# The reciprocal root of 24 RMS norms: a square root on ScalarE and a reciprocal on VectorE for a logarithm and an exponential

## The reference

```
def rms_norm(x, g):
    xf = x.astype(jnp.float32)
    y = xf * lax.rsqrt(jnp.mean(xf * xf, axis=-1, keepdims=True) + EPS)
    return (y * g.astype(jnp.float32)).astype(x.dtype)
...
    o = rms_norm(o, g_out) * jax.nn.silu(r.reshape(B, L, GLA_HEADS, GLA_DV).astype(jnp.float32))
...
    for l in range(DEPTH):
        a = rms_norm(h, p['g_mix_pre'][l])
...
        h = h + rms_norm(m, p['g_mix_post'][l])
...
        f, c_new = conv_ffn(rms_norm(h, p['g_ffn_pre'][l]), prev, p['w_up'][l], p['conv_w'][l],
                            p['conv_b'][l], p['w_down'][l])
        new_conv.append(c_new)
        h = h + rms_norm(f, p['g_ffn_post'][l])
```

## Time and profile before

| | us |
|---|---|
| median of 3 runs | 2798.29 |
| lowest and highest | 2792.39, 2800.5 |
| profiled execution | 2794.6 |
| its span | 2792.8 |

### The profile page before, as it was taken

The page is one execution under the profiler, slowest core; times in us unless marked ns, Lnnn a source line. Parts: engine busy times, 40 slices in busy tenths (PEclk is TensorE's granted clock), DMA queues, the critical chain, the costliest instruction groups (busy, mean ns, idle before and its releaser), DMA issues.

```text
span 2792.8 us, 37637 instructions
## 1 busy us (share of the span) xinstructions
PE 2521.1 (90%) x15437; PEld 2206.9 (79%) x15437; DVE 1654.8 (59%) x2811; ACT 1140.4 (41%) x1792; POOL 85.5 (3%) x22
## 2 busy tenths in 40 slices
PE   2999999998999999999997889878999999999994
PEld 1777888887778879999995666667777888999994
DVE  2677556665665555765555666665665555655554
ACT  2555444343443324333334656553443333333232
POOL 0000000000010000010000110000001000000000
PEclk8999999988999999999998899989999999999997
DMA  7222213322422323323223222221332232332222
GB/s 153 78 67 76 84 63 101 106 85 81 155 78 96 98 76 96 133 74 99 84 84 100 74 90 76 67 93 34 107 129 91 93 98 79 106 118 80 88 91 75
DMA packets 93799, 255.17 MB, mean 91 GB/s; under 512 B 10947, under 2 KB 44204, under 8 KB 91820
## 3 DMA queue, kind: packets, MB, share of 16 engines
q1 hardware_dynamic: 69916, 209.24, 24.1%
q10 hardware_dynamic: 23712, 43.52, 4.4%
HBM read 225.92 MB, written 26.74 MB: 90 GB/s over the span
## 4 chain that ended last, share of the span: by engine, by line
PE 39%; DVE 5%; ACT 4%; issue 3%; DMA 1%; POOL 1%; ACTq 0%; DVEq 0%
PE banks L431 23%; PE banks L451 13%; DMA normed<-h_scratch 1%; ACT w_hi L409 1%; DVE w_lo L414 1%; PE banks L1569 1%; PE banks L1543 1%; ACT probs L1860 1%; PE banks L1555 1%; POOL act_lo L574 1%; DVE normed L561 0%; ACT act_hi L570 0%; DVE hf L1371 0%; DVE stats L1724 0%; ACT normed L488 0%
## 5 line engine op out<-in xcount | busy, mean ns | idle before, releaser
L431 PE MATMUL banks<-act_hi,w_lo 128*128 128x272 f32 (+1 forms) x2952 | 977.1, 331 | 49.5 <-DVE act_lo L574 21.1
L431 PE MATMUL banks<-act_hi,w_hi 128*128 128x272 f32 (+1 forms) x2952 | 963.1, 326 | 0.0
L431 PE MATMUL banks<-act_lo,w_hi 128*128 128x272 f32 (+1 forms) x2952 | 961.8, 326 | 0.0
L409 ACT ACTIVATE w_hi<-w_raw 128x1024 fp32r<-128x1024 f32 x366 | 380.5, 1055 | 778.8 <-PE banks L451 518.4
L414 DVE TENSOR_TENSOR w_lo<-w_raw,w_hi 128x1024 fp32r<-128x1024 f32 x366 | 464.8, 1283 | 375.9 <-ACT w_hi L409 375.7
L431 PEld LDWEIGHTS banks<-act_hi,w_lo 128*128 128x128 f32 x2952 | 562.5, 191 | 112.9 <-issue 27.4
L431 PEld LDWEIGHTS banks<-act_lo,w_hi 128*128 128x128 f32 x2952 | 563.5, 191 | 44.0 <-issue 1.7
L431 PEld LDWEIGHTS banks<-act_hi,w_hi 128*128 128x128 f32 x2952 | 561.7, 190 | 44.0
L463 DVE TENSOR_TENSOR acc<-acc,banks 128x272 f32<-128x272 f32 (+1 forms) x624 | 315.9, 518 | 216.5 <-PE banks L451 212.5
L451 PE MATMUL banks<-h_hi,w_lo 128*128 128x272 f32 (+1 forms) x1056 | 354.9, 336 | 59.0 <-issue 36.1
L451 PE MATMUL banks<-h_lo,w_hi 128*128 128x272 f32 (+1 forms) x1056 | 351.4, 333 | 0.0
(11 more groups left out here) (209 smaller groups left out, 2657.8 us busy)
## 6 DMA issues: line engine op xcount, KB each, us to landing
w_raw<-wall SPq DMA_DIRECT2D x366, 512.0 KB, 3.6
normed<-h_scratch ACTq DMA_DIRECT2D x12, 704.0 KB, 4.7
h_scratch<-acc ACTq DMA_DIRECT2D x3, 2176.0 KB, 8.5
h_scratch<-acc ACTq DMA_DIRECT2D x3, 2048.0 KB, 8.3
gstates<-state ACTq DMA_DIRECT2D x4, 1024.0 KB, 6.2
gla_s<-gstates ACTq DMA_DIRECT2D x4, 1024.0 KB, 4.0
bias<-bias_scratch SPq DMA_DIRECT2D x32, 128.0 KB, 3.6
bias_scratch<-bias_rows SPq DMA_DIRECT2D x1, 3064.0 KB, 36.6
```

The costliest lines, as they stand in the source:

```text
L409: nc.scalar.activation(WH[:, b % RING], WR[:, b % RAW], ACT.Copy).then_inc(w_hi, 1)
L431: last = nc.tensor.matmul(PS[:, bank, 0:n], w, a[X][:, k, o:o + n], start=(k == 0 and first), stop=(k == KT - 1 and w is wh and a is AH))
```

## The change

EPSC, the tile that holds eps, gets a second column. `act_rstd` becomes `act_root`: a square root of one column of EPSC into the other, without any wait, then the wait for ss_done, then the square root of mean + eps (ms_done). A new `dve_reciprocal` on VectorE waits for ms_done, takes the reciprocal of RS[X] in place and raises rs_done; it is called at the head of `dve_post` (m = 0, first pair) and of `dve_norm` (m = 0, all but "mix"). The eight GLA head norms get the same in line. Line numbers behind the edits move up by 7 to 11.

```diff
@@ -206,7 +206,7 @@
         WL = place("w_lo", [P, RING, KT * P], fp32r)
         ident = place("ident", [P, P])
         ones = place("ones", [P, P])
-        EPSC = place("eps_col", [P, 1])
+        EPSC = place("eps_col", [P, 2])
         GC = place("gain_cols", [P, NGAIN])
         SINK = place("sinks_b", [P, NQ])
         arena = at[0]
@@ -509,12 +509,17 @@
                 last = nc.tensor.matmul(PS[:, bank + c, 0:w_], ones[:], RS[X][:, o:o + w_], start=True, stop=True)
             last.then_inc(ss_done, 1)
 
-        def act_rstd(act, i, kind, X, bank):
+        def act_root(act, i, kind, X, bank):
+
             n = NORMS[i, kind, X]
+            nc.scalar.activation(EPSC[:, 1:2], EPSC[:, 0:1], ACT.Sqrt)
             act.wait_ge(ss_done, n)
-            nc.scalar.activation(like(X, RS[X][:]), banks(X, bank), ACT.Ln, bias=EPSC[:], scale=1.0 / D).then_inc(ms_done, 1)
-            act.wait_ge(ms_done, n)
-            nc.scalar.activation(RS[X][:], RS[X][:], ACT.Exp, scale=-0.5).then_inc(rs_done, 1)
+            nc.scalar.activation(like(X, RS[X][:]), banks(X, bank), ACT.Sqrt, bias=EPSC[:, 0:1], scale=1.0 / D).then_inc(ms_done, 1)
+
+        def dve_reciprocal(dve, i, kind, X):
+            n = NORMS[i, kind, X]
+            dve.wait_ge(ms_done, n)
+            nc.vector.reciprocal(RS[X][:], RS[X][:]).then_inc(rs_done, 1)
 
         def act_h_load(act, i, X, m):
 
@@ -537,6 +542,8 @@
         def dve_post(dve, i, X, m, pairs=(0, 1)):
 
             p = POSTS[i, X]
+            if m == 0 and pairs[0] == 0:
+                dve_reciprocal(dve, i, "post", X)
             dve.wait_ge(rs_done, NORMS[i, "post", X])
             for y in pairs:
                 a = ACC[X][:, m * KH + 2 * y:m * KH + 2 * y + 2]
@@ -552,6 +559,8 @@
 
         def dve_norm(dve, i, kind, X, m):
             a = ACTS[i, kind, X]
+            if m == 0 and kind != "mix":
+                dve_reciprocal(dve, i, kind, X)
             dve.wait_ge(rs_done, NORMS[i, "kv" if kind == "mix" else kind, X])
             if m:
                 dve.wait_ge(al_done, 2 * a - 1)
@@ -587,7 +596,7 @@
             if step in (0, 1):
                 act_square(act, i, "post", X, step)
             elif step == 2:
-                act_rstd(act, i, "post", X, bank)
+                act_root(act, i, "post", X, bank)
                 act_h_load(act, i, X, 0)
             elif step == 3:
                 act_h_load(act, i, X, 1)
@@ -597,7 +606,7 @@
                 if step == 4 and i:
                     act_h_store(act, i, X)
             elif step == 6:
-                act_rstd(act, i, kind, X, bank)
+                act_root(act, i, kind, X, bank)
             elif step in (7, 8):
                 act_hi(act, i, kind, X, step - 7)
 
@@ -1039,6 +1048,8 @@
                 nc.vector.tensor_tensor(SQ0[:, 0, 0:W], SQ0[:, 0, 0:W], SQ0[:, 1, 0:W], ALU.add).then_inc(gq_f, 1)
                 if more:
                     rest_after(dve, ("k", u + 1))
+                dve.wait_ge(gq_ms, u + 1)
+                nc.vector.reciprocal(RS0[:, 0:W], RS0[:, 0:W]).then_inc(gq_rs, 1)
                 dve.wait_ge(gq_rs, u + 1)
                 for d in range(2):
                     nc.vector.scalar_tensor_tensor(O[:, d, 0:W], O[:, d, 0:W], col(G_GLA + d), RS0[:, 0:W],
@@ -1216,10 +1227,9 @@
                 nc.scalar.activation(SQ0[:, :, 0:W], O[:, :, 0:W], ACT.Square).then_inc(gq_sq, 1)
                 act.wait_ge(r_ev, VR[u, 1, len(CHUNKS[X]) - 1])
                 nc.scalar.activation(R[:, :, 0:W], R[:, :, 0:W], ACT.Silu).then_inc(gq_si, 1)
+                nc.scalar.activation(EPSC[:, 1:2], EPSC[:, 0:1], ACT.Sqrt)
                 act.wait_ge(gq_ss, u + 1)
-                nc.scalar.activation(like(X, RS0[:, 0:W]), banks(X, 2), ACT.Ln, bias=EPSC[:], scale=1.0 / DV).then_inc(gq_ms, 1)
-                act.wait_ge(gq_ms, u + 1)
-                nc.scalar.activation(RS0[:, 0:W], RS0[:, 0:W], ACT.Exp, scale=-0.5).then_inc(gq_rs, 1)
+                nc.scalar.activation(like(X, RS0[:, 0:W]), banks(X, 2), ACT.Sqrt, bias=EPSC[:, 0:1], scale=1.0 / DV).then_inc(gq_ms, 1)
                 if more:
                     values_done(u + 1, 0)
                 if X:
@@ -2115,7 +2125,7 @@
 
         @block.vector
         def _(dve):
-            nc.vector.memset(EPSC[:], EPS)
+            nc.vector.memset(EPSC[:, 0:1], EPS)
             nc.vector.memset(ones[:], 1.0).then_inc(one, 1)
             nc.vector.memset(TBL[:], 1.0).then_inc(tb_one, 1)
             dve.wait_ge(rb_full, 1)
@@ -2144,7 +2154,7 @@
             w_round(act, 0)
             act_square(act, 0, "pre", 0, 1)
             w_round(act, 1)
-            act_rstd(act, 0, "pre", 0, 2)
+            act_root(act, 0, "pre", 0, 2)
             act_hi(act, 0, "pre", 0, 0)
             w_round(act, 2)
             act_hi(act, 0, "pre", 0, 1)
```

## The result

The changed kernel takes 2828.97 us, the median of four executions from 2819.28 to 2838.53, against 2798.4 for the kernel before: a ratio of 1.0108 with a 95% interval of 1.0091 to 1.0126, so 30.6 us slower. The forecast was 2850 in a range of 2805 to 2895.

What follows compares the result with a forecast made beforehand. TensorE was taken as the bound, a norm costing only where TensorE runs dry behind it. From the profiled 2794.6 us, 45.2 for later norm results and 10.5 for slow clock gave 2850, range 2805 to 2895.

Steps and rivals of the forecast that it cites:

- R: Time of VectorE's wide reciprocal: 4.5 us for 512 columns, 4.8 for 544, half of the upper price per column.
- straight line: Between fast divide and forecast, time rises 15.4 us per us of reciprocal, from -15.7 at 0.7; turning point 1.7.
- GLA heads: Head norms of turns 0 to 7, whose results TensorE's down products wait for: +20.7 us, 11.0 of it in turns 0 to 3.
- Reciprocals in a full queue: Norms in turns 7 and 1 and two in attention, where VectorE is busy anyway and pays the reciprocal: +12.8 us together.
- ConvFFN, step 2: Post norm of the other half, four times: earlier transfer of h hides 1.73 us, 1.2 stays each: +4.7 us.
- ConvFFN, step 6: Pre or kv norm of the other half, three times, ahead of L414's weights, nothing covering it: +9.0 us.
- Attention, step 2: Post norms beside attention, twice: the earlier transfer of h gains more than the later result costs: -3.0 us.
- The end: Final norm: L549 late by 1.2 us after the earlier transfer of h, less the dummy's 0.2: +1.0 us.
- The clock: Seven TensorE gaps grown to 3.5 to 4.5 us, each followed by slow clock costing 1.5: +10.5 us.
- Returned table loads: 15 loads come back ahead of exponentials in GLA and attention; only turn 4's counted, +1.3 us.
- the rival of the fast divide: One-pass reciprocal of 0.7 us makes results 1.05 us earlier: sum -15.7, so 2779 us; chance 0.13.
- The change doesn't do what it says: Rival: 67 table loads for 76, not 52; near no change, 2792 to 2802 for reciprocals of 1.5 to 2.2 us; chance 0.05.

Runs made afterwards that it cites:

- one pass: Changed kernel with a one-pass minimum with 1.0 in place of each wide reciprocal, so no division and other numbers: 2792.8 us, ratio 0.9978 against the kernel before.
- no dummy: Changed kernel without its dummy square root of one column: 2825.51 us, ratio 1.0092 against the kernel before.
- exponential early: Changed kernel with a one-column exponential behind each head's square root, loading that table early: 2824.92 us, ratio 1.0089; the same on the minimum-for-reciprocal kernel: 2784.83 us.
- layers only: Kernel before with square root and reciprocal in the sixteen layer norms only, the eight GLA head norms as before: 2811.02 us, ratio 1.0051.
- heads only: Kernel before with square root and reciprocal in the eight GLA head norms only, the sixteen layer norms as before: 2812.82 us, ratio 1.0051.
- half divide: Changed kernel with the reciprocal on half of the tokens and a one-pass minimum on the others: 2801.4 us, ratio 1.0003 against the kernel before.
- load late: Changed kernel with the old wait for the root's end put back ahead of step 2's load of h: 2833.17 us, ratio 1.0119 against the kernel before.
- filled: Changed kernel with six overwritten matmuls on TensorE while it waits for the head norm in GLA turns 0 to 2: 2828.13 us, ratio 1.0108.

## Why the prediction was right, and where its steps were off

The direction and the mechanism held: a reciprocal on VectorE longer than what ScalarE is spared, in front of things that TensorE waits for. Step by step:

- **R**, the term that was mis-sized. 4.5 and 4.8 us were taken, 3.35 and 3.55 measured, and a result is 1.6 to 1.8 us later, not 2.75 to 3.0. The bounds of 0.7 and 8.9 held it; halving the upper price was the choice that failed, by a quarter. Put into the prediction's own straight line, which holds no new slow clock, R = 3.45 would give -15.7 + 15.4 x 2.75 = +27, or 2821. So R alone is more than the 21 us between 2850 and 2829; of the 8 us from 2821 to 2829, 3.8 are the base, since the sum started from an execution of before that is faster than the median. (The forecast's rise over its base is 55.7 us; 30.6 were measured.) That +27 comes close to 30.6 is luck in part: the same line gives -20 for the one pass, where 5 to 6 us less were measured.
- **GLA heads**: right in kind. TensorE's gap in front of the down products grew by 1.47 in turns 0 and 2, not 2.75, and the stretch of turns 0 to 3 cost 7.9 where 12.3 was said (11.0, and 1.3 for the other norm in turn 1), and 18.3 with the clock. Turns 4 to 7 cost 21.7 in the profiled execution, more than the 14.2 forecast for them, but 12 of that is granted clock, and the traces of no dummy and exponential early have 14.6 and 10.5 there.
- **Reciprocals in a full queue**: L522 pays its 3.35 us in full in turn 7, where it follows its predecessor without idle time, and the gap of 4.50 us is behind it:

```profile
626.29 3.35 DVE L522 RECIPROCAL rstd<-rstd 128x512 f32<-128x512 f32 x1
...
633.98 0.80 PE L763 MATMUL banks<-gat,gv 128*128 128x128 f32 x2 [4.50 <-DVE gstate_steps L1034]
```

  The kv norm of attention cost 4.9 between 1562 and 1612 where 4.8 was said, and that with a smaller R; layers only has the same 4.8 there, and one pass -0.6. The other norm of attention, 2.2 said, can't be read out: heads only, which doesn't change it, moves by 1.9 in the same place.
- **ConvFFN, step 2**: 4.7 said, nothing measured. The working was right: 1.73 us of waiting for the transfer is gone, and with the real R the root is 1.7 later, so they cancel.
- **ConvFFN, step 6**: 3 x 3.0 said; 1.76 more idle time and a shift of 1.7 at f = 0; at f = 1 a shift of 1.5 that the next wait takes back within 10 us; 3.0 at f = 2, where 1.4 is granted clock. Together 4.7 for 9.0: "Nothing covers it" does not hold at f = 1.
- **Attention, step 2**: -3.0 said, -1.1 and -1.5 in the shifts. The end: +1.0 said, 0.
- **The clock**: 1.5 us a gap was right in size (1.7), but not as time lost: in turn 2 nearly nothing of it is left. Seven new gaps over 3 us were said; the trace has two of these in turns 0 and 2. In turn 3 it is 2.44 and at f = 0 and 2 of step 6 2.31, as R is smaller; turn 1 has 1.44, less than the 1.71 of before. The fall of 41 us in turn 7 was not counted, though the kernel before has one of 17 in the same place.
- **Returned table loads**: counted as 1.3 us in turn 4 and nothing elsewhere. The wait of VectorE has it in the profiled execution (2.73 for 1.32), though not in each (1.20 in heads only), and turn 6 has it too (2.74 for 1.33). Some eight us in the one-pass kernel hung on them, so the rival of the fast divide was too good by that: 2779 was said, 2792.8 measured.
- **"The change doesn't do what it says"** was right in what it counts, 24 loads gone and 15 back, and the sum's own step that an early load brings nothing was right too: the dummy is worth nothing. Its price, 2792 to 2802 for an R of 1.5 to 2.2, is what half divide measured.

What stays open: why most of the price comes only above R = 2.0. The traces show slow clock in the stretches where it does (37.0 us of it from 340 to 680 after, 29.7 with the half divide, 28.9 with one pass, 25.1 before), but the changed kernel's variants with the whole divide have 29.2 to 31.5 there (no dummy, load late, filled, exponential early), so most of the step from 29.7 to 37.0 is this one execution, and the one test of the clock did not keep TensorE busy as it was meant to. Open too is what decides whether a gap of TensorE is followed by half clock.

Two small slips in the prediction's fast-divide sum (five results 1.05 us earlier are 5.25 and not 5.1, three gaps of 0.55 are 1.65 and not 1.5) change nothing.

## What to carry to other kernels

Before work is moved from one engine to another, the moved operation has to be timed at its own width; two narrow rows of it, 157 and 164 ns, said nothing of the 3.35 us of the wide one. A table load removed at one place comes back ahead of the next activation of another set, so the whole loop's sequence of functions decides, not the pair that is edited. And an instruction in front of a DMA issue is a wait for the DMA: one transposed line, with nothing computed differently, was worth 16 to 19 us where the rewritten norm cost 31. Last, one trace is one execution: the 6.8 us in attention could be told from the change only because other kernels' traces were laid beside it.

## What the hardware showed that was not expected

- VectorE's reciprocal in float32: 1749 ns for 256 columns, 1851 for 272, 3350 for 512, 3551 for 544. From 256 to 512 that is (3350 - 1749) / 256 = 6.25 ns for each column, and about 0.15 us besides. The estimate from the Trainium skill ("VectorE: DVE Perf Modes", section "First, the fixed hardware budget", a repeat count of 8) was 4.3 us for 512 columns and is too long. An estimate from the clock of 0.96 GHz that the same page gives (section "Specifications"): the measured 6.25 ns are 6 cycles a column.
- The table load showed 1283 ns and no drain behind it: in the changed kernel the dummy starts at 126.43, 0.02 us after the load's end at 126.41, and where nothing is waited for it is as short behind the loads of every trace. By the Trainium skill ("ScalarE: Activation LUTs", section "What ACT_TABLE_LOAD costs") it would be 1.38 us later. The measurement decides.
- TensorE's clock stayed at 1.2 GHz (0.50) for the 26 us from 632 to 658, while TensorE was busy for 22.81 of them, and on to 673, 41 us in all. And one and the same list gave two gaps in front of one matmul, 1.89 us in layers only, where TensorE came to it at half clock, and 4.50 in the changed kernel, where it came at full clock.
